# One weight chunk of a mixture-of-experts stage fetched by sixteen transfers of eight rows in place of one of 128 rows

## The reference, cut to what matters

```
def moe_swiglu(x, w_router, w1, w3, w2):
    logits = (xf @ w_router).astype(jnp.float32)
    top_vals, top_idx = lax.top_k(logits, TOP_K)            # 2 of 8 experts for each token
    gates = jax.nn.softmax(top_vals, axis=-1)
    ...
    def block_fn(args):
        tok, e = args
        xb = xf[tok]
        return (jax.nn.silu(xb @ w1[e]) * (xb @ w3[e])) @ w2[e]
    ...
    y = y * gate_buf[:, None].astype(y.dtype)
    out = jax.ops.segment_sum(y, tok_buf, num_segments=n)
```

## Time and profile before

| | |
|---|---|
| median of three runs | 1808.28 us |
| the profiled execution | 1808.6 us |
| its span, first to last instruction | 1806.7 us |
| PE busy | 1742.4 us, 96% of the span |
| DVE busy | 1004.4 us, 56% |
| ACT busy | 774.0 us, 43% |
| SP's own queue of transfers (q1) | 499.50 MB, 69.9% of the time of 16 DMA engines |
| transfers from `w_moe` | 336 (224 to ring, 75 to arena, 37 to row) of 1024 KB |

### The profile page before, as it was taken

How to read it: one execution, slowest core, us unless ns; L and a number is a source line. 1 busy time by engine, 2 the same in 40 slices (tenths; PEclk the granted TensorE clock), 3 DMA queues, 4 the chain that set the end, 5 groups by cost and what they waited for, 6 DMA issues and landing times.

```text
span 1806.7 us, 31172 instructions
## 1 busy us (share of the span) xinstructions
PE 1742.4 (96%) x13166; PEld 1350.7 (75%) x13166; DVE 1004.4 (56%) x1222; ACT 774.0 (43%) x995; POOL 128.3 (7%) x102
## 2 busy tenths in 40 slices
PE   9999999999999999999999999999999999999886
PEld 8987889777888899989878777777555566665542
DVE  6867643458767665577676777886322233332102
ACT  7766533345346433334635555665222233320001
POOL 0033000000102220000200001200000000000000
PEclk9999999999999999999999999999999999999899
DMA  6532464423572655548329999999999999999996
GB/s 257 196 119 94 163 233 163 163 96 123 205 266 71 250 187 187 188 163 270 131 102 408 418 420 412 421 421 420 421 413 421 420 421 420 420 420 420 421 420 256
DMA packets 76171, 515.73 MB, mean 285 GB/s; under 512 B 8816, under 2 KB 12144, under 8 KB 15488
## 3 DMA queue, kind: packets, MB, share of 16 engines
q1 hardware_dynamic: 72128, 499.50, 69.9%
q0 software_dynamic: 3296, 13.17, 2.1%
q10 hardware_dynamic: 608, 1.07, 0.2%
HBM read 509.11 MB, written 1.05 MB: 282 GB/s over the span
## 4 chain that ended last, share of the span: by engine, by line
PE 79%; DMA 9%; DVE 6%; ACT 3%; issue 2%; POOL 0%; DVEq 0%; SPq 0%; ACTq 0%
PE bank L800 69%; DMA ring<-in_w_moe 5%; DMA arena<-in_w_moe 4%; ACT whi L2390 1%; DVE wrest L3322 1%; DVE whi L3322 1%; PE bank L1581 1%; PE bank L1015 1%; PE bank L1703 1%; DVE wrest L2447 1%; PE bank L1379 1%; PE bank L903 0%; PE bank L1018 0%; PE bank L1602 0%; PE bank L1692 0%
## 5 line engine op out<-in xcount | busy, mean ns | idle before, releaser
L800 PE MATMUL bank<-ring,arena 128*32 128x128 f32 (+2 forms) x2984 | 193.6, 319 | 6.8 <-DMA ring<-in_w_moe 6.3
L2390 ACT ACTIVATE whi<-ring 128x2048 fp32r<-128x2048 f32 x80 | 151.9, 1915 | 71.2 <-DMA ring<-in_w_moe 66.1
L800 PEld LDWEIGHTS bank<-ring,arena 128*32 128x32 f32 (+1 forms) x2984 | 121.9, 120 | 80.4 <-issue 42.0
L800 PE MATMUL bank<-hTh,wrest 128*128 128x256 f32 x608 | 170.1, 280 | 0.0
L3322 DVE TENSOR_TENSOR wrest<-ring,whi 128x2048 fp32r<-128x2048 f32 x55 | 131.0, 2398 | 36.2 <-ACT whi L2390 35.9
L2447 DVE TENSOR_TENSOR wrest<-ring,fhi 128x2048 fp32r<-128x2048 f32 x33 | 76.9, 2331 | 80.3 <-ACT fhi L1862 80.2
L800 PEld LDWEIGHTS bank<-hTh,wrest 128*128 128x128 f32 x608 | 114.2, 188 | 0.0
L3322 DVE TENSOR_TENSOR whi<-ring,whi 128x2048 fp32r<-128x2048 f32 x25 | 57.3, 2293 | 86.6 <-ACT whi L2390 86.6
L800 PE MATMUL bank<-whi,hidE 128*128 128x512 f32 x264 | 91.4, 405 | 8.3 <-DVE hidR L3275 8.3
L800 PE MATMUL bank<-hTh,fhi 128*128 128x256 f32 x352 | 98.5, 280 | 0.0
L3322 DVE TENSOR_TENSOR whi<-arena,whi 128x2048 fp32r<-128x2048 f32 x27 | 61.8, 2290 | 66.0 <-ACT whi L2390 66.0
(11 more groups left out here) (579 smaller groups left out, 4387.7 us busy)
## 6 DMA issues: line engine op xcount, KB each, us to landing
ring<-in_w_moe SPq DMA_DIRECT2D x224, 1024.0 KB, 11.8
ring<-in_w_dense SPq DMA_DIRECT2D x135, 1024.0 KB, 4.8
arena<-in_w_moe SPq DMA_DIRECT2D x75, 1024.0 KB, 12.1
row<-in_w_moe SPq DMA_DIRECT2D x37, 1024.0 KB, 11.4
row<-in_rows POOLq DMA_DIRECT2D x17, 512.0 KB, 5.6
arena<-arena SPq DMA_DIRECT2D x32, 106.5 KB, 4.1
arena<-in_tbias POOLq DMA_DIRECT2D x2, 1536.0 KB, 8.8
h<-in_x SPq DMA_DIRECT2D x2, 512.0 KB, 4.8
```

The costliest lines, as they stand in the source:

```text
L800: ins = pe.matmul(out_, lhsT, rhs, start=start, stop=stop, **more)
L2390: S["w_hi"].on(a.activation(late_hi(b), late_raw(b), ACT.Copy))
```

## The change

A constant names position 240. A new function `parts(m)` gives 16 for it and 1 for every other position. Where SP issued one transfer for a chunk, it now issues `parts(m)` of them, each for an equal run of rows, each adding 16 to the semaphore of the place. `late_count` adds 16 for each transfer beyond the first that the same semaphore has seen so far, so that all who wait for chunk 240, or for a later chunk in its place, wait for all sixteen transfers. Everything else is as it was.

```
+EIGHT_ROWS_AT = 240
...
+        def parts(m):
+
+            return P // 8 if m == EIGHT_ROWS_AT else 1
+
         def late_count(m):
 
             k, first = m // LATE_RING, PLACE_ORDER[m % LATE_RING]
-            return 16 * ((N_DENSE + first) // RING + 1 if first < RING else 2) + 16 * k
+            more = sum(parts(n) - 1 for n in range(m % LATE_RING, m + 1, LATE_RING))
+            return 16 * ((N_DENSE + first) // RING + 1 if first < RING else 2) + 16 * (k + more)
...
-                sp.dma_start(late_raw(m), w_moe[bass.ds(ids[rank] * E_CHUNKS + in_expert(step % E_STEPS, c), 1)]
-                             .rearrange("a p n -> p (a n)")).then_inc(late_ready(m), 16)
+                to = late_raw(m)
+                chunk = w_moe[bass.ds(ids[rank] * E_CHUNKS + in_expert(step % E_STEPS, c), 1)].rearrange("a p n -> p (a n)")
+                for n in range(parts(m)):
+                    rows_ = slice(n * P // parts(m), (n + 1) * P // parts(m))
+                    sp.dma_start(to[rows_, :], chunk[rows_, :]).then_inc(late_ready(m), 16)
```

## The result

Six runs of the changed kernel have a median of 1817.62 us (1816.05 to 1817.76), six of the kernel before of 1808.43. The ratio is 1.0048, with a 95% interval of 1.0038 to 1.0058: 9.2 us slower. The forecast was 1806.2, with a range up to 1811.6.

What follows compares the result with a forecast made beforehand. The DMA chunk stream was taken as the bound: early engines end at 1787.7 (+2.63), late ones at 1787.3 (-2.50), the later 2.1 us before 1789.8, so 1808.3 - 2.1 = 1806.2 us; own range 1805.1 to 1807.4, 8-in-10 range 1805.0 to 1811.6.

Steps and rivals of the forecast that it cites:

- The stream sets the end: Chunk stream at 420 GB/s: its last landing sets the time, with 15.8 us of work on the last chunk behind it.
- SP hides its issues: Sixteen issues at 0.6 us each send position 241 out at 1545.3; the queue hides this with 3.4 us to spare: 0 us.
- Rival 3: SP too slow at position 240: at 1.03 us per issue the late engines idle 3.5 us; +1.0, 1809.3; chance 0.07.
- Semaphore writes cost next to nothing: Chunk 240's short transfers: 9 ns per semaphore write, so fifteen more add 0.14 us on each loaded engine.
- Short transfers overlap: Chunk 240's sixteen transfers overlap, as sixteen of 106.5 KB in the trace did, landing 3.9 us after issue, issued every 0.70 us.
- Rival 4: Chunk 240's short transfers do not overlap on an engine: 40 us, of which the queue hides 14; about 1834; chance 0.03.
- 0.95 us for each 64 KB: The skill page's price for small transfers: sixteen one after another an estimated 15 us instead of 2.5; set aside for the trace.
- A loaded engine pays 0.312 us for a row: Chunk 240: eight more rows on each loaded engine cost +2.50 us, with semaphore writes +2.63; spared engines gain 2.50.
- The loaded eight are the early eight: Chunk 240's short transfers load the eight engines that finish early, ending them at 1787.7 instead of 1785.1; chance 0.52.
- late eight: Stream's tail: eight of sixteen DMA engines work on 4.7 us after the others, to 1789.8; spared, they end at 1787.3.
- rival 1: Chunk 240's short transfers load the late eight, which end 2.63 us later: 1810.9, slower; chance 0.28.
- wrong altogether: Sign for the whole forecast: a change over 3 us either way, or an unchanged tail with another time; stream's end not deciding.

Runs made afterwards that it cites:

- the first series: Against the kernel before, chunk 240 as 16 x 8 rows four apart at both ends (+4.8 us), chip only (+6.1), source only (+9.3), or 8 x 16 rows (+6.7).
- rows 0 to 63 by eights: Against the kernel before, only rows 0 to 63 of chunk 240 fetched, as eight transfers of eight rows four partitions apart, rows 64 to 127 left out: 1807.85 us.

## Why the prediction was wrong, point by point

- **The stream sets the end: right.** The last landing came 7.4 us later and the 15.8 us behind it stayed.
- **SP hides its issues: right.** The pitch was 0.46 us (but for the first issue, which alone took 0.96), under my lowest bound of 0.53, and 241 went out at 1543.2, 2.1 us earlier than the 1545.3 that I took; q1 stayed above 100%. Rival 3 falls here. In the first series, where the pitch was 0.84, the engines did run dry.
- **Semaphore writes cost next to nothing: right.** With eight times as many as an ordinary chunk on each engine that wrote, rows 0 to 63 by eights lost no time.
- **Short transfers overlap: right.** Rival 4 and, beside it, 0.95 us for each 64 KB fall with the run of rows 0 to 63. The page has that price from transfers that GpSimd issued. I set that rule aside rightly; the one that mattered, the map of partitions to engines told above, I did not weigh.
- **A loaded engine pays 0.312 us for a row: wrong, and the step that failed.** I took a row's price from the earlier trace rows, where every engine writes its own partitions, and asked only how many rows each engine gets, not where they go. The rows took 0.55 us, and not on the loaded engines alone: all sixteen, on ordinary rows too, for some 15 us. By the count of semaphore writes (179 beside 523 rows) the 128 short rows all fall between 1543 and 1559 us, the length of the hole. No rival of mine had it. The splits with an even load give it nearly by itself: 8 x 16, 4 x 32 and 2 x 64 rows cost 5.8 to 6.8 us.
- **The loaded eight are the early eight: wrong.** Had they been, the run of rows 0 to 63, which spares the other eight 2.5 us, would have ended 2.5 us earlier (1806.0). It came out at 1807.85, and its time alone (-0.7; the ratio's interval is -2.7 to +0.5) doesn't decide; the tail does, 1783 to 1799 us:

```profile
DMA  5565565433311101000000000000000000000000
GB/s 246 225 266 225 225 266 225 184 143 143 143 61 61 61 41 61 20 41 20 0 0 0 0 0 0 0 0 0 0 0 0 0 0 0 0 0 0 0 0 0
```

  From 1787.4 on the rate is 20 to 61 GB/s: two engines, then one, which end near 1790.5, about where the late eight of the earlier trace rows ended. So most of the late eight were spared and ended earlier, and about two of them were loaded; the count of short rows above, six engines early and two late, says the same. In the change these two have +2.63 us, the price of rival 1, and set the end. Rival 1 had this size right, though not all eight: two late engines are enough. What misled me was the earlier trace rows: from one fetch beside six first packets I concluded for all late engines; and that fetches are what makes engines late no run shows. I also misread the end of the earlier trace rows by one slice: the last packets start at 1790.0 to 1790.4, which moves the late end by 0.4 us and no conclusion.
- **The sum, corrected.** 5.8 to 6.8 us for the hole (the even splits) and 2.6 for the two late engines are 8.4 to 9.4; measured 9.2. The second term was not measured alone; 9.2 less the even splits leaves 2.4 to 3.4 for it.
- **The width.** My range rested on rivals that all kept a row's price. Of what I had named as wrong altogether, the change of more than 3 us came true, but not for the reason that I gave with it: the stream's end still sets the time.

No version tried beats the kernel before. Sparing the late engines could give at most the few us of the earlier trace rows, and rows 0 to 63 alone, with eight engines spared, did not show a gain that can be told from none.

## What to carry to other kernels

Ask of each split of a transfer not only how many engines it uses and how many bytes each gets, but whether each engine still writes the partitions that it has in the full transfer. Cut a chunk by columns, with all 128 partitions in each part (four parts: +0.3 us, interval -1.6 to +1.6), and not by partitions (two parts: +6.8). In this stream, which its DMA engines bound, one such split slowed what was in flight beside it, and nothing later gave the time back.

## What was not expected of the hardware

- One chunk split by partitions held all sixteen engines at 188 to 336 GB/s, against 420, for 11 to 17 us in the runs where no engine ran dry, although only 1 MB was split, and the loss was of one size whether in 2, 4, 8 or 16 parts (4.8 to 7.0 us of rate).
- By the count of semaphore writes, two engines that write into partitions of others were enough to hold all sixteen at 205 to 254 GB/s.
- All engines stayed busy in that time: the busy share of the DMA engines shows nothing of it, the rate does.
- SP's issue of eight rows that lie four partitions apart took 0.84 us from one to the next, against 0.46 for contiguous ones, also for contiguous rows on the chip whose source rows lie apart.
- Transfers of all partitions with 2 KB pieces nearly kept the rate (381 to 434 GB/s in the slices where they ran).
